# Expert products of a mixture block: every second unit of keys and values in fp32, the others with 400 and 200 columns, 56 gathered tokens, values in two passes

## The reference, cut to what matters

```python
def peer(u, w_q, keys_1, keys_2, expert_u, expert_v):
    q = (tok @ w_q).reshape(ntok, PEER_HEADS, 2, PEER_DQ // 2)
    ...                                  # scores, two top_k of 16, top_k of the 256 sums
    experts = e1 * PEER_NKEYS + e2
    gates = jax.nn.softmax(top, axis=-1).astype(u.dtype)
    def block(args):
        xb, eb, gb = args
        ue = jnp.take(expert_u, eb, axis=0)
        act = jax.nn.gelu(jnp.einsum('nhkd,nd->nhk', ue, xb), approximate=False) * gb
        return jnp.einsum('nhk,nhkd->nd', act, jnp.take(expert_v, eb, axis=0))
```

## Time and profile before

| | |
|---|---|
| median of 3 runs | 2376.14 us |
| profiled execution | 2374.39 us, span of its trace 2372.6 us |
| granted TensorE clock | 0.997 of full speed |
| busy: TensorE, VectorE, ScalarE, POOL | 99%, 64%, 57%, 35% |
| DMA packets | 499.5 MB, mean 211 GB/s |

### The profile page before, as it was taken

How to read it: one execution, slowest core, us unless ns; L and a number is a source line. 1 busy time by engine, 2 the same in 40 slices (tenths; PEclk the granted TensorE clock), 3 DMA queues, 4 the chain that set the end, 5 groups by cost and what they waited for, 6 DMA issues and landing times.

```text
span 2372.6 us, 51129 instructions
## 1 busy us (share of the span) xinstructions
PE 2338.8 (99%) x19066; PEld 2203.6 (93%) x19066; DVE 1526.2 (64%) x2468; ACT 1340.8 (57%) x2369; POOL 830.7 (35%) x612
## 2 busy tenths in 40 slices
PE   9999999999999999999999999999999999999998
PEld 8888787978888789999999999999999999999998
DVE  5568988557566565675667877776456566666534
ACT  5456554255544545777776666666555555555555
POOL 0000201100000002445556545554556566666554
PEclk9999999999999999999999999999999999999999
DMA  7665554046666557666778766675777777777684
GB/s 215 186 195 151 160 168 152 22 128 193 194 195 215 169 182 230 193 199 220 240 260 283 255 216 233 227 242 165 259 252 248 266 248 256 260 256 262 226 256 147
DMA packets 197218, 499.52 MB, mean 211 GB/s; under 512 B 14726, under 2 KB 82824, under 8 KB 187656
## 3 DMA queue, kind: packets, MB, share of 16 engines
q1 hardware_dynamic: 187719, 430.20, 57.1%
q0 software_dynamic: 9408, 68.16, 8.2%
HBM read 491.98 MB, written 5.24 MB: 210 GB/s over the span
## 4 chain that ended last, share of the span: by engine, by line
PE 92%; DVE 3%; ACT 2%; DMA 1%; POOL 1%; issue 1%; SPq 0%; ACTq 0%
PE PS L920 19%; PE PS L923 10%; PE PS L518 9%; PE PS L867 9%; PE PS L868 9%; PE PS L871 9%; PE PS L561 5%; PE PS L563 5%; PE PS L562 5%; PE PS L520 4%; PE PS L511 3%; PE PS L879 2%; DVE w_lo L1437 1%; POOL big L1364 1%; DMA raw<-in_w_out 0%
## 5 line engine op out<-in xcount | busy, mean ns | idle before, releaser
L958 ACT ACTIVATE w_hi<-raw 128x512 fp32r<-128x512 f32 x1576 | 985.6, 631 | 919.9 <-PE PS L923 291.3
L1437 DVE TENSOR_TENSOR w_lo<-raw,w_hi 128x512 fp32r<-128x512 f32 x1064 | 748.3, 715 | 759.1 <-ACT w_hi L958 757.1
L1392 POOL TENSOR_TENSOR w_lo<-raw,w_hi 128x512 fp32r<-128x512 f32 x512 | 707.7, 1392 | 1095.4 <-ACT w_hi L958 1089.3
L920 PE MATMUL PS<-act_both,w_hi 128*128 128x224 f32 x4096 | 540.5, 274 | 0.0
L920 PEld LDWEIGHTS PS<-act_both,w_hi 128*128 128x128 f32 x4096 | 498.5, 192 | 0.2 <-DVE act_both L2083 0.2
L867 PE MATMUL PS<-act_both,w_hi 128*128 128x224 f32 x2048 | 489.0, 277 | 3.6 <-ACT big L1239 3.6
L868 PE MATMUL PS<-act_both,w_hi 128*128 128x224 f32 x2048 | 483.2, 274 | 0.0
L867 PEld LDWEIGHTS PS<-act_both,w_hi 128*128 128x128 f32 x2048 | 393.0, 192 | 4.3 <-issue 4.3
L868 PEld LDWEIGHTS PS<-act_both,w_hi 128*128 128x128 f32 x2048 | 393.1, 192 | 0.0
L518 PE MATMUL PS<-act_both,w_hi 128*128 128x512 f32 x1056 | 373.2, 400 | 6.9 <-DVE w_lo L1437 6.1
L923 PE MATMUL PS<-act_both,w_lo 128*128 128x224 f32 x2048 | 312.1, 275 | 0.3 <-POOL w_lo L1392 0.2
(11 more groups left out here) (261 smaller groups left out, 1930.6 us busy)
## 6 DMA issues: line engine op xcount, KB each, us to landing
raw<-in_peer_u_t SPq DMA_DIRECT2D x256, 512.0 KB, 4.3
raw<-in_peer_v SPq DMA_DIRECT2D x256, 512.0 KB, 4.7
raw<-in_w_in SPq DMA_DIRECT2D x180, 512.0 KB, 3.8
raw<-in_w_out SPq DMA_DIRECT2D x32, 512.0 KB, 4.5
raw<-in_peer_w_q SPq DMA_DIRECT2D x32, 512.0 KB, 4.3
raw<-in_w_ret_branch SPq DMA_DIRECT2D x16, 512.0 KB, 4.4
raw<-in_w_rwkv_branch SPq DMA_DIRECT2D x16, 512.0 KB, 4.5
big<-in_x SPq DMA_DIRECT2D x2, 1024.0 KB, 5.9
```

Source lines behind the costliest of these rows:

```text
L920: pe.matmul(v_bank(j), w_hi[:, k % 2, cols], act2[:, b, w, :], start=first and j % 2 == 0 and w == 0, stop=False)
L958: act.activation(w_hi[:, slot % 2, hh * 512:(hh + 1) * 512], raw[:, slot, hh * 512:(hh + 1) * 512], ACT.Copy).then_inc(S["unit_hi"], 1)
L1392: pool.tensor_tensor(w_lo[:, k % 2, cols], raw[:, k, cols], w_hi[:, k % 2, cols].bitcast(f32), ALU.subtract).then_inc(S["p_split"], 1)
L1437: dve.tensor_tensor(w_lo[:, slot % 2, cols], raw[:, slot, cols], w_hi[:, slot % 2, cols].bitcast(f32), ALU.subtract).then_inc(S[done], 1)
```

## The change

- Units `k` = 1 and 3 of each four are no longer split. TensorE multiplies them in fp32 straight from `raw` (line 902 of the new kernel for keys, 967 for values), with fp32 copies of the moving operand: `x32` for the keys (made once, by POOL, from high and low part), `v32` for the values (copied by ScalarE). Their slot is loaded again only after TensorE has finished the unit (`half_used`).
- Units `k` = 0 and 2 are split as before, ScalarE and POOL only, and the two matmuls with the high part become one with 2 x 200 columns: high and low part of the tokens beside each other, into 400 columns of a bank. The low part adds 200 columns. The two halves of the bank are summed afterwards by VectorE (`usum` for the keys, ahead of the gelu, which now works in place).
- The layout of units and pairs follows: in the keys a block is still two units, but one of each kind.
- 56 tokens instead of 32 are gathered, in two groups of 56 rows per gather instead of four of 32, so 64 gathers of 112 rows per stage instead of 32 of 128. 200 tokens remain for the full products, 25 turns of gates instead of 28. The gathers and their uses are placed by unit (`USED_UNIT`, `LEAD`), the choice of experts for the first half is due at turn 9 instead of 13, and SP sends the indices at turn 11 instead of 15.
- The values go in two passes `h` over all 128 blocks, 1024 channels each, one unit per block; each pass has one channel group of 400 columns per bank. Between the passes the banks are emptied (`sum_tile` on VectorE, `odd_out` on ScalarE and a sum on POOL). The last units of a pass go bank by bank (`last_units`).

```diff
-U_SPLIT = {"p_split": (0, 2), "d_split": (1, 3)}
-V_SPLIT = {"p_split": (0, 2), "d_split": (1, 3)}
+U_ROUNDED, V_ROUNDED = (0, 2), (0, 2)
...
-SPARSE = 32
+SPARSE = 56
 DT = TOK - SPARSE
+GROUPS = 2
+ROWS = GROUPS * SPARSE
...
+EARLY_DOTS = (4 * GATE_AT - 52) * 5 // 9
+DOT_UNIT = [52 + 9 * t // 5 for t in range(EARLY_DOTS)]
+DOT_UNIT += [4 * GATE_AT + (4 * GATE_TURNS - 3) * t // (2 * PICK_TILES - EARLY_DOTS) for t in range(2 * PICK_TILES - EARLY_DOTS)]
+MAC_UNIT = [264 + 208 * t // (2 * PICK_TILES - 1) for t in range(2 * PICK_TILES)]
+USED_UNIT = DOT_UNIT + MAC_UNIT
+LANDS, LEAD = 3, 6
+IDS_AT, ADD_AT, FINAL_AT = 11, 120, 24
...
             def load_u(it):
                 for k in range(4):
...
+                    elif k in U_ROUNDED:
+                        sp.wait_ge(*split_done("u", it - 1, k, 2))
                     else:
-                        sp.wait_ge(*split_done("u", it - 1, k, 2))
+                        sp.wait_ge(S["half_used"], it * 8 + 2 * (U0 + k - 3))
...
             def um(it, k):
 
-                out = PS[:, 4 + k // 2, 0:DT]
+                bank = 4 + k // 2
                 for hh in range(2):
                     if k % 2 == 0 and hh == 0:
 
-                        wait_past(pe, S[f"gelu{k // 2}"], it)
-                    pe.wait_ge(S["unit_hi"], it * 8 + (2 * U0 + 2 * k + hh + 1))
-                    chunks = [((k % 2) * 8 + 4 * hh + c, slice((4 * hh + c) * P, (4 * hh + c + 1) * P)) for c in range(4)]
-                    for kc, cols in chunks:
-                        pe.matmul(out, w_hi[:, k % 2, cols], act_hi[:, kc, SPARSE:TOK], start=kc == 0, stop=False)
-                        pe.matmul(out, w_hi[:, k % 2, cols], act_lo[:, kc, SPARSE:TOK], start=False, stop=False)
-                    pe.wait_ge(*split_done("u", it, k, hh + 1))
-                    for kc, cols in chunks:
-                        last = pe.matmul(out, w_lo[:, k % 2, cols], act_hi[:, kc, SPARSE:TOK], start=False, stop=kc == 15)
+                        wait_past(pe, S[f"gelu{k // 2}"], 2 * it - 1)
+                    chunks = [(4 * hh + c, slice((4 * hh + c) * P, (4 * hh + c + 1) * P)) for c in range(4)]
+                    if k in U_ROUNDED:
+                        pe.wait_ge(*hi_done("u", it, k, hh + 1))
+                        for c, cols in chunks:
+                            pe.matmul(pair_bank(bank), w_hi[:, k // 2, cols], act_both[:, c, :, SPARSE:TOK], start=c == 0, stop=False)
+                        pe.wait_ge(*split_done("u", it, k, hh + 1))
+                        for c, cols in chunks:
+                            last = pe.matmul(PS[:, bank, 0:DT], w_lo[:, k // 2, cols], act_hi[:, c, SPARSE:TOK], start=False, stop=False)
+                    else:
+                        if hh == 0:
+                            pe.wait_ge(S[f"raw_in{k}"], it * 16 + 16 * (U0 // 4 + 1))
+                        for c, cols in chunks:
+                            last = pe.matmul(PS[:, bank, 0:DT], raw[:, k, cols], x32[:, c, :], start=False, stop=c == 7)
                     last.then_inc(S["half_used"], 1)
...
+            def last_units(h):
...
+                it = BLOCKS // 4 - 1
+                for j in range(8):
...
+                    pe.matmul(pair_bank(j), w_hi[:, 1, cols], act2[:, 1], start=False, stop=False)
...
+                    last = pe.matmul(PS[:, j, 0:DT], w_lo[:, 1, cols], act2[:, 1, 0, :], start=False, stop=False)
...
+                    last = pe.matmul(PS[:, j, 0:DT], raw[:, 3, cols], v32[:, 1, :], start=False, stop=True)
+                    last.then_inc(S["tile_done"], 1)
+                    if h == 1 and j in (2, 4, 6):
+                        turn_rows((j - 2) // 2)
...
             def late_gelu(i, b):
 
-                act.wait_ge(S["half_used"], i * 8 + (2 * U0 + 8 * GATE_AT + 4 * b + 4))
-                if not (isinstance(i, int) and i == 0):
-                    act.wait_ge(S["late"], i * 2 + (b - 1))
-                act.activation(late_out[b], PS[:, 4 + b, 0:DT], ACT.Gelu).then_inc(S[f"gelu{b}"], 1)
+                act.wait_ge(S[f"gelu{b}"], 2 * i + (2 * GATE_AT + 1))
+                act.activation(late_out[b], late_out[b], ACT.Gelu).then_inc(S[f"gelu{b}"], 1)
...
+            for c in range(8):
+                pool.tensor_tensor(x32[:, c, :], act_hi[:, 8 + c, SPARSE:TOK].bitcast(f32), act_lo[:, 8 + c, SPARSE:TOK].bitcast(f32),
+                                   ALU.add).then_inc(S["x32"], 1)
...
+            def usum(it, b, late=True):
+
+                dve.wait_ge(S["half_used"], it * 8 + (2 * U0 + 4 * b + 4))
+                dve.tensor_reduce(late_out[b] if late else G[:, 2 * it + b, :], summed(4 + b), AX.X, ALU.add).then_inc(S[f"gelu{b}"], 1)
```

More of the change, by code:

```diff
@@ L335, in rot_table, with rounded, hi_done @@
             return cst[:, col:col + TOK].unsqueeze(1).unsqueeze(1).broadcast_to([P, 2, 2, TOK])
+        def rounded(stage, it, k, halves):
+            of = U_ROUNDED if stage == "u" else V_ROUNDED
+            before = 0 if stage == "u" else UPAIRS * 2 * len(U_ROUNDED)
+            return it * (2 * len(of)) + (before + 2 * of.index(k) + halves)
+        def hi_done(stage, it, k, halves):
+            return S["unit_hi"], rounded(stage, it, k, halves) + 2 * U0
         def split_done(stage, it, k, halves):
[L339 to L342, removed]
+            return S["p_split"], rounded(stage, it, k, halves)
         def unit_slot(ku, j, kq):
@@ L497, in _ @@
+            for it in range(FINAL_AT + 6, BLOCKS // 4):
+                load_v(1, it)
             for tt in range(2):
@@ new lines, in vm @@
+            def vm(h, it, k, first=False):
+                if k in V_ROUNDED:
+                    pe.wait_ge(S["act2_split"], it * 2 + (h * (BLOCKS // 2) + k // 2 + 1))
+                else:
+                    pe.wait_ge(S["act2_hi"], it * 4 + (h * BLOCKS + k + 1))
+                    pe.wait_ge(S[f"raw_in{k}"], it * 16 + 16 * ((V0 + h * BLOCKS) // 4 + 1))
+                for hh in range(2):
+                    tiles = [(4 * hh + t, slice((4 * hh + t) * P, (4 * hh + t + 1) * P)) for t in range(4)]
+                    if k in V_ROUNDED:
+                        pe.wait_ge(*hi_done("v", it + h * (BLOCKS // 4), k, hh + 1))
+                        for j, cols in tiles:
+                            if first:
+                                bank_free(h, j)
+                            pe.matmul(pair_bank(j), w_hi[:, k // 2, cols], act2[:, k // 2], start=first, stop=False)
+                        pe.wait_ge(*split_done("v", it + h * (BLOCKS // 4), k, hh + 1))
+                        for j, cols in tiles:
+                            last = pe.matmul(PS[:, j, 0:DT], w_lo[:, k // 2, cols], act2[:, k // 2, 0, :], start=False, stop=False)
+                    else:
+                        for j, cols in tiles:
+                            last = pe.matmul(PS[:, j, 0:DT], raw[:, k, cols], v32[:, k // 2, :], start=False, stop=False)
+                    last.then_inc(S["half_used"], 1)
@@ L950, in _, with v_blocks @@
+            for h in range(2):
+                def v_blocks(it, first=False, final=False):
+                    for k in range(2 if final else 4):
+                        vm(h, it, k, first and k == 0)
+                    if final:
+                        last_units(h)
+                v_blocks(0, first=True)
+                with pe.Fori(1, BLOCKS // 4 - 1) as it:
+                    v_blocks(it)
+                v_blocks(BLOCKS // 4 - 1, final=True)
         @block.scalar
@@ L2014, in gate_turn @@
                 for par in range(2):
+                    usum(i + (GATE_AT - 1), par, not first)
                     if not first:
                         gate_in(i - 1, par)
+                    sparse_step(4 * (i + GATE_AT) + 2 * par)
                     if not final:
@@ L2076, in _ @@
                 gate_turn(i)
[L2077 to L2088 removed]
+            usum(BLOCKS // 2 - 1, 0)
```

388 lines of the change are left out of this document (205 added, 183 removed).

## The result

The changed kernel takes 2426.5 us (median of 4 runs, 2422.2 to 2428.8) against 2376.3 us before: the ratio is 1.021, 95% interval 1.020 to 1.023. It is slower, clear of the noise, where 2311 us was forecast. Its profiled execution has a span of 2420.4 us.

The account below looks back on a forecast made before the run. TensorE, busy 99% of the span, was taken as the bound: 2374.4 - 79.9 (units) - 5.5 (gates) + 20 (late loads) + 2 (end) = 2311 us; range 2272 to 2368.

Parts of the forecast that it names:

- Part 1: TensorE's units in keys and values: four cost 10.10 us against 10.72, taking 79.9 us off (75 to 100).
- part 4: Transfers of loads and gathers: the bytes fit, but late loads of fp32 units add 20 us (0 to 60).
- 213 ns "and about 3 more": TensorE's 256-column fp32 pass: two 2.4 GHz clock periods per column plus 3 ns, giving 169.5 ns at 200 columns.
- Rival A: Short matmuls have no floor, 200 columns cost 102 ns: 2293 us, or 2273 with no late loads (chance 0.13).
- Part 2: Gate matmuls: turns fall from 28 to 25, each adding 1.82 us, so 5.5 us off.
- Part 3: Work moved off TensorE to VectorE, ScalarE and POOL: no engine is full, so it costs nothing.
- Rival D: TensorE waits for VectorE's sum, chained with ScalarE's gelu and gating, in 50 half turns: 2336 to 2361 us (chance 0.04).
- Part 5: Start, middle and end: nothing between the two values passes, +2 us (0 to 4) after the last unit.
- Rival C: Slower than before: the queues do not sustain the mix, TensorE goes at the bytes' speed; 2424 us at 275 GB/s (chance 0.09).
- Rival B: Late loads cost two to three times the 20 us taken: 2335 to 2368 us (chance 0.15).
- the fast 10 us of before: The old kernel's fastest 10 us of transfers: 326 GB/s at busy share 0.93, taken as 350 at full share.
- The test that I wrote down: Signs in TensorE's timeline and waits: fp32 matmuls wait some 20 us for transfers; waits past 60 us mean transfers were misjudged.

Follow-up runs that it names:

- e1: The changed kernel without the 128 gathers of rows; VectorE multiplies the tokens' own rows and waits for no landing: 2296.0 us, ratio 0.968 to the kernel before.
- e5: The changed kernel with 64 of the 112 rows of every gather fetched, landing in the even partitions: 2301.7 us, ratio 0.968 to the kernel before.
- e3: The changed kernel with every gather fetching 128 rows instead of 112, the last 16 unused: 2343.0 us, ratio 0.988 to the kernel before.
- e2: The changed kernel with only rows 0 to 63 of every gather's 112 fetched, into partitions 0 to 63: 2365.1 us, ratio 0.996 to the kernel before.

## Why the prediction was wrong

Part 1, the unit, held: 5.07 us a pair against 5.05, and e1, which has all of it, is at 2296.0 us where the sum without part 4 was 2291. The units' split, 2.65 and 2.42 us where 2.71 and 2.34 were forecast, is off by 0.06 and 0.08 and cancels, but it depends on reading the weight loads: in TensorE's own timeline above sixteen fp32 passes take 2.89 us with a last record of 0.33, so they follow each other every 171 ns, close to the forecast 169.5. The forecast's 213 ns "and about 3 more" at 256 columns rests on the row of 216 alone; the other row, 209, lies under 213. Only the pair is firm, and its 0.02 us too much make the 5 us over 256 pairs. Rival A is out: no lower floor is seen.

Part 2 held: in e1 line 910's weight loads run from 1320.3 to 1607.3 us for 25 turns, 11.96 us a turn (forecast 11.9). Four units without gates are 10.14 us, so the gates add 1.82, as forecast.

Part 3 held: in e1 TensorE is busy for 499.99 of 500 us of the values stage and all 300.00 us from 1300 to 1600, with all of VectorE's work in place and POOL's but for the gathers; in e5, which issues these too, it is busy for 499.29 of 500 us. Rival D is out.

Part 5 is not tested apart; e1 leaves no room for more than a few us.

Part 4 failed. It is after less e1, 130 us, where I took 20 with a bound of 60. The failing step is "So the bytes fit, with little room", from which the term of 20 us for late loads follows: it set a demand in bytes (320 GB/s) against a rate (350 at full share) that had been reached with gathers of 128 rows, and took that rate over to gathers of 112. For gathers of 128 rows that rate was nearly there, as e3 shows: 316 GB/s held over 500 us, and 2343 us. With 112 rows the same engines gave 269. Of the 130 us, at least 83 are the slow rows (after less e3, although e3 moves more bytes); the other 47 us are what gathers of 128 rows at their faster price cost (e3 less e1), still over twice my 20, but within the bound.

Two more steps in it were wrong. It counted late loads of fp32 units alone. TensorE's waits for these are 19.7 us, just the 20 that I took; the 53.3 us at the rounded units (1.3 in e1), whose loads pass through ScalarE and POOL before TensorE can begin, were not in the sum.

And a late load was priced at the wait, with some of it "taken back". The runs show the reverse. From 930 us on TensorE's waits add up to 3 us in e1, 24 in e3, 45 in e2 and 75 in after; the profiled executions took 2294.4, 2334.3, 2368.6 and 2422.2 us. So over e1 waits of 21, 42 and 72 us came with 40, 74 and 128 us, about twice as much. In after the clock is a part of this: 0.985 of full over the span against 0.996, some 27 us. In e3 it is not, its clock is 0.997. The rest was not taken apart; a matmul record includes its way through the pipeline, so that part of a wait can stand as busy time.

Rival C had the outcome: it said 2424 us if the queues gave 275 GB/s, and they gave 269 in the values stage and 2426 us. That the time fits so well is luck in part, since the 275 was picked and not read from a row. Its reason, that the queues do not sustain the mix, holds for gathers of 112 rows alone; with 128 they moved 316. Rival B, late loads at two to three times my 20 us, is where the kernel with fast rows (e3, 2343 us) would stand; the real one is past it. C got 0.09 since the fast 10 us of before spoke against it, and those had another form of gather. The test that I wrote down pointed at the right part: the waits passed 60 us (75), though the fp32 units' share of them was the 20 us that it named.

What stays open is the map from a gather's rows to engines and partitions that makes 64, 112 and 120 rows slow (587, 486, 581 ns) and 128 fast. That 112 rows are 7 for each of 16 engines, and so lie across groups of 8 partitions, fits the slow 112 and the fast 128 but was not shown: only for 64 rows did a run change the partitions alone, and the profile names neither engine nor partition of a packet. Gathers of 120 rows did not come near the 2335 to 2345 us expected of 15 engines with 8 rows each.

## What to carry to other kernels

Where gathers run beside a stream of loads, gather full sets of 128 rows, even if some rows are thrown away, or spread fewer rows over the partitions (shown for 64 rows in the even ones); before cutting rows from a transfer, compare the queue's engine time per byte, since bytes and share of the DMA engines can move in opposite directions. A measured rate holds only for the form of transfer that it was measured on. And price a wait of TensorE at about twice the length that the profile gives it (1.8 to 1.9 times here), at full clock too.

## What I had not expected of the hardware

- The same 64 rows of 8 KB cost 587 ns each in partitions 0 to 63 and 360 ns in the even ones (e2, e5).
- 112, 120 and 128 rows per gather: 486, 581 and 346 ns a row, 2426, 2600 and 2343 us.
- After waits of 1.87 and 1.99 us, sixteen fp32 passes of 200 columns took 4.66 and 4.50 us instead of 2.89; the granted clock was 0.62 in the mean over the 9 us around the second.
- Queues at a share of 0.99 moved 296 GB/s with rows of 112 and, at 0.88, 316 GB/s with rows of 128: the busy share does not say how near the limit is.
